# Gate weights' sums by adding DMAs issued by GpSimd instead of VectorE additions

## The reference, cut to what matters

```python
proj = jnp.einsum('bsd,df->bsf', h, w_in[l])          # h: 512 x 2048
gates = jax.nn.sigmoid(parts[9 + 3 * n_g] + gate_b[l]) # the last 3 * 2048 columns of proj
```

## Time and profile before

| what | value |
|---|---|
| median of three runs | 2642.93 us |
| the profiled execution's own time | 2641.48 us |
| its span | 2639.7 us |
| TensorE busy | 2616.3 us (99%) |
| VectorE busy | 1554.9 us (59%) |
| ScalarE busy | 866.8 us (33%) |
| GpSimd busy | 0.2 us |
| share of PE in the chain that ended last | 95% |
| DMA | 359.41 MB, 136 GB/s over the span |

### The profile page before, as it was taken

One profiled execution on the slowest core, in us unless ns is written; L12 is line 12 of the kernel. 1 busy time (PEld: TensorE's weight loads), 2 busy tenths in 40 slices (PEclk: granted clock), 3 DMA queues, 4 the chain that ended last, 5 costly groups with the idle time before them and its releaser, 6 DMA issues.

```text
span 2639.7 us, 31265 instructions
## 1 busy us (share of the span) xinstructions
PE 2616.3 (99%) x12030; PEld 2162.5 (82%) x12030; DVE 1554.9 (59%) x1911; ACT 866.8 (33%) x1089; POOL 0.2 (0%) x4
## 2 busy tenths in 40 slices
PE   9999999999999999999999999999999999999998
PEld 7888888888888888888888888878888888888776
DVE  7653654554455455365455446798877784444775
ACT  6222332322222233232232223334444443212454
POOL 0000000000000000000000000000000000000000
PEclk9999999999999999999999999999999999999999
DMA  6333333332332432333334243435455436444565
GB/s 220 120 92 126 97 118 97 120 124 91 124 132 84 131 116 89 112 108 123 93 120 131 84 132 124 139 114 186 168 190 177 164 131 247 160 144 143 189 190 195
DMA packets 102825, 359.41 MB, mean 136 GB/s; under 512 B 10017, under 2 KB 10274, under 8 KB 100770
## 3 DMA queue, kind: packets, MB, share of 16 engines
q1 hardware_dynamic: 82352, 296.49, 34.2%
q10 hardware_dynamic: 20338, 60.89, 6.3%
HBM read 317.50 MB, written 39.85 MB: 135 GB/s over the span
## 4 chain that ended last, share of the span: by engine, by line
PE 95%; DVE 3%; DMA 1%; issue 1%; SPq 0%; ACT 0%; DVEq 0%; ACTq 0%
PE proj L421 22%; PE proj L423 22%; PE proj L422 22%; PE sc_ps L421 3%; PE sc_ps L422 3%; PE sc_ps L423 3%; PE tr_ps L421 3%; PE tr_ps L422 3%; PE tr_ps L423 3%; PE o_ps L422 2%; PE o_ps L423 2%; PE o_ps L421 2%; PE tr_ps L462 2%; PE sc_ps L454 1%; DVE w_lo L1019 1%; PE o_ps L507 1%
## 5 line engine op out<-in xcount | busy, mean ns | idle before, releaser
L421 PE MATMUL proj<-act_hi,w_hi 128*128 128x512 f32 x2304 | 908.1, 394 | 0.5 <-DVE stage L1146 0.2
L423 PE MATMUL proj<-act_hi,w_lo 128*128 128x512 f32 x2304 | 898.2, 390 | 0.0
L422 PE MATMUL proj<-act_lo,w_hi 128*128 128x512 f32 x2304 | 897.2, 389 | 0.0
L1015 DVE TENSOR_TENSOR w_lo<-raw,w_hi 128x1024 fp32r<-128x1024 f32 x288 | 352.7, 1225 | 396.4 <-ACT w_hi L703 395.9
L703 ACT ACTIVATE w_hi<-raw 128x1024 fp32r<-128x1024 f32 x288 | 304.6, 1058 | 837.3 <-PE proj L423 832.3
L423 PEld LDWEIGHTS proj<-act_hi,w_lo 128*128 128x128 f32 x2304 | 432.5, 188 | 91.4
L421 PEld LDWEIGHTS proj<-act_hi,w_hi 128*128 128x128 f32 x2304 | 432.8, 188 | 89.2 <-issue 1.1
L422 PEld LDWEIGHTS proj<-act_lo,w_hi 128*128 128x128 f32 x2304 | 433.0, 188 | 86.3
L1019 DVE TENSOR_TENSOR w_lo<-raw,w_hi 128x1024 fp32r<-128x1024 f32 x152 | 185.7, 1223 | 219.2 <-ACT w_hi L707 218.9
L707 ACT ACTIVATE w_hi<-raw 128x1024 fp32r<-128x1024 f32 x152 | 161.2, 1061 | 353.3 <-PE proj L423 149.9
L707 ACT ACTIVATE w_hi<-kb 128x1024 fp32r<-128x1024 f32 x120 | 127.2, 1061 | 185.8 <-PE proj L423 65.4
(11 more groups left out here) (297 smaller groups left out, 3354.5 us busy)
## 6 DMA issues: line engine op xcount, KB each, us to landing
raw<-wst SPq DMA_DIRECT2D x288, 512.0 KB, 3.5
raw<-wg SPq DMA_DIRECT2D x48, 512.0 KB, 4.0
raw<-wb SPq DMA_DIRECT2D x48, 512.0 KB, 3.6
kb<-wg SPq DMA_DIRECT2D x10, 2048.0 KB, 7.6
ssum<-wo ACTq DMA_DIRECT2D x8, 2048.0 KB, 10.5
s_dram<-ssum ACTq DMA_DIRECT2D x8, 2048.0 KB, 7.5
raw<-s_dram SPq DMA_DIRECT2D x32, 512.0 KB, 3.4
kb<-wg SPq DMA_DIRECT2D x24, 512.0 KB, 5.9
```

The costliest lines, as they stand in the source:

```text
L421: nc.tensor.matmul(out, w_h, a_h, start=first, stop=False, skip_group_check=shared)
L422: nc.tensor.matmul(out, w_h, a_l, start=False, stop=False, skip_group_check=shared)
L423: return nc.tensor.matmul(out, w_l, a_h, start=False, stop=last, skip_group_check=shared)
L1015: tt(w_lo[slot_w][:, :], raw[slot_raw][:, :], w_hi[slot_w][:, :].bitcast(f32), ALU.subtract).then_inc(lo_done, 1)
```

## The change

The three areas become two. `sum_a` (at the place of the old `k1`) is loaded with W22; GpSimd then issues DMAs that add a unit of a weight from HBM onto it in place: W21 (giving R1), after R1's split W11 (R2), after R2's split W12 (R4). `sum_b` (at the place of the old `k3`) is loaded with W21, and W11 is added (R3). These are 16 adding DMAs of 512 KB a quad, 96 in all, and VectorE's 96 additions are gone. W11, the operand of product 0, comes through the ring, so the ring carries 12 units a quad in place of 8. All loads are now single units of 512 KB; the first quad's are issued by SP behind `o_ready`, `sum_a` and `sum_b` ahead of the ring, and ScalarE issues none.

```diff
+RING_G = 3 * NU
+X_B = RING_G * QUADS_G
...
-def summed(kind, q, u):
-    return 16 * q + 4 * kind + u + 1
+def summed(kind, q):
+    return 16 * {R1: 3 * q + 1, R2: 3 * q + 2, R4: 3 * q + 3, R3: q + 1}[kind]
...
-        k2, k3, k1 = [[kb[:, 4096 * n + HU * u:4096 * n + HU * (u + 1)] for u in range(NU)] for n in range(3)]
+        sum_a, sum_b = [[kb[:, 4096 * n + HU * u:4096 * n + HU * (u + 1)] for u in range(NU)] for n in (2, 1)]
...
                 elif x < X_B + RING:
-                    q, n = divmod(x - RING, 8)
-                    if n < NU:
-                        sp.wait_ge(sum_done, summed(R4, q, n))
-                    else:
-                        sp.wait_ge(lo_done, R_G + STEPS * q + 24 + n - NU + 1)
+                    q, n = divmod(x - RING, RING_G)
+                    sp.wait_ge(lo_done, R_G + STEPS * q + 12 * (n // NU) + n % NU + 1)
...
             for u in range(NU):
-                load_k1(0, u)
+                load_a(0, u)
+            for u in range(NU):
+                load_b(0, u)
             for q in range(QUADS_G):
-                for u in range(3):
-                    load_12(q, u)
+                for n in range(NU):
+                    load_part(q, n, W11)
                 if q:
                     sp.wait_ge(got, evicted(q - 1, 6, 1))
                 sp.dma_start(rows[:, 0:2 * C], rows_d[0:1, 2 * C * q:2 * C * (q + 1)].to_broadcast([P, 2 * C])).then_inc(brow_in, 16)
-                sp.wait_ge(sum_done, summed(R2, q, NU - 1))
-                if q < QUADS_G - 1:
-                    sp.dma_start(kb[:, 0:4096], wg[q + 1, W22, :, :]).then_inc(k2_in, 16)
-                else:
+                for n in range(NU, 2 * NU):
+                    load_part(q, n, W12)
+                if q == QUADS_G - 1:
                     for b in range(3):
                         sp.wait_ge(y_stored[b], 16 * (HEADS + 1))
                     load_y(0)
-                load_12(q, 3)
-                for u in range(3):
-                    load_22(q, u)
+                for n in range(2 * NU, 3 * NU - 1):
+                    load_part(q, n, W22)
                 if q < QUADS_G - 1:
-                    sp.wait_ge(lo_done, R_G + STEPS * q + 20)
-                    sp.dma_start(kb[:, 4096:8192], wg[q + 1, W21, :, :]).then_inc(k3_in, 16)
+                    for u in range(NU):
+                        sp.wait_ge(lo_done, R_G + STEPS * q + 16 + u + 1)
+                        load_b(q + 1, u)
                     for u in range(NU):
                         sp.wait_ge(lo_done, R_G + STEPS * q + 20 + u + 1)
-                        load_k1(q + 1, u)
-                load_22(q, 3)
+                        load_a(q + 1, u)
+                load_part(q, 3 * NU - 1, W22)
...
+        @block.gpsimd
+        def _(pool):
+            def sum_units(q, kind):
+                buf, part, done = {R1: (sum_a, W21, a_sum), R2: (sum_a, W11, a_sum), R4: (sum_a, W12, a_sum), R3: (sum_b, W11, b_sum)}[kind]
+                for u in range(NU):
+                    if kind == R1:
+                        pool.wait_ge(a_in[u], 16 * (q + 1))
+                    elif kind == R3:
+                        pool.wait_ge(b_in[u], 16 * (q + 1))
+                    else:
+                        pool.wait_ge(lo_done, R_G + STEPS * q + {R2: NU, R4: 2 * NU}[kind] + u + 1)
+                    pool.dma_start(buf[u], wg[q, part, :, HU * u:HU * (u + 1)], accum_op=ALU.add).then_inc(done[u], 16)
+
+            for q in range(QUADS_G):
+                sum_units(q, R1)
+                sum_units(q, R2)
+                sum_units(q, R3)
+                sum_units(q, R4)
...
-                    if n < 4:
-                        add_units(R3, q, n)
-                    if 4 <= n < 8:
-                        add_units(R2, q, n - 4)
-                    if 12 <= n < 16:
-                        add_units(R4, q, n - 12)
-                    if 24 <= n and q < QUADS_G - 1:
-                        add_units(R1, q + 1, n - 24)
```

More of the change, by code:

```diff
@@ L62 @@
 R_O = R_B + GROUPS * NU
-X_B = 8 * QUADS_G
+RING_G = 3 * NU
+X_B = RING_G * QUADS_G
 X_O = X_B + GROUPS * NU
@@ L244, in program @@
         raw_in = [sem(f"raw_in{i}") for i in range(RING)]
-        k1_in = [sem(f"k1_in{i}") for i in range(NU)]
-        k2_in, k3_in = sem("k2_in"), sem("k3_in")
+        a_in, b_in = [[sem(f"{n}_in{i}") for i in range(NU)] for n in "ab"]
+        a_sum, b_sum = [[sem(f"{n}_sum{i}") for i in range(NU)] for n in "ab"]
         brow_in, grow_in = sem("brow_in"), sem("grow_in")
@@ L267, in program @@
         th_ready, sq_ready, sd_ready, y_ready = sem("th_ready"), sem("sq_ready"), sem("sd_ready"), sem("y_ready")
-        sum_done, got, gate_done = sem("sum_done"), sem("got"), sem("gate_done")
+        got, gate_done = sem("got"), sem("gate_done")
         comb_sum, comb_hi, comb_lo = sem("comb_sum"), sem("comb_hi"), sem("comb_lo")
@@ L318, in ring_free, with load_part, load_a, load_b @@
                 elif x < X_B + RING:
-                    q, n = divmod(x - RING, 8)
-                    if n < NU:
-                        sp.wait_ge(sum_done, summed(R4, q, n))
-                    else:
-                        sp.wait_ge(lo_done, R_G + STEPS * q + 24 + n - NU + 1)
+                    q, n = divmod(x - RING, RING_G)
+                    sp.wait_ge(lo_done, R_G + STEPS * q + 12 * (n // NU) + n % NU + 1)
                 else:
                     sp.wait_ge(lo_done, R_B + x - RING - X_B + 1)
[L327 to L336, removed]
+            def load_part(q, n, kind):
+                ring_free(RING_G * q + n)
+                load_ring(RING_G * q + n, wg[q, kind, :, HU * (n % NU):HU * (n % NU + 1)])
+            def load_a(q, u):
+                sp.dma_start(sum_a[u], wg[q, W22, :, HU * u:HU * (u + 1)]).then_inc(a_in[u], 16)
+            def load_b(q, u):
+                sp.dma_start(sum_b[u], wg[q, W21, :, HU * u:HU * (u + 1)]).then_inc(b_in[u], 16)
             def load_y(b):
@@ L716, in hi_g @@
                 r = R_G + STEPS * q + n
[L717 to L722, removed]
+                if p == 1:
+                    act.wait_ge(a_sum[u], summed(R1, q))
+                    hi_of(r, sum_a[u])
                 elif p == 2:
-                    act.wait_ge(sum_done, summed(R2, q, u))
-                    hi_of(r, k1[u])
+                    act.wait_ge(a_sum[u], summed(R2, q))
+                    hi_of(r, sum_a[u])
                 elif p == 4:
-                    act.wait_ge(sum_done, summed(R3, q, u))
-                    hi_of(r, k3[u])
+                    act.wait_ge(b_sum[u], summed(R3, q))
+                    hi_of(r, sum_b[u])
                 elif p == 5:
-                    act.wait_ge(sum_done, summed(R4, q, u))
-                    hi_of(r, k1[u])
+                    act.wait_ge(a_sum[u], summed(R4, q))
+                    hi_of(r, sum_a[u])
                 else:
-                    hi_ring(r, 8 * q + (u if p == 3 else NU + u))
+                    hi_ring(r, RING_G * q + NU * (p // 3) + u)
             def comb_high(n, dst, src, ready):
@@ L839, in head @@
                         exps(i, 4 + w - 10, sc, [(0, 6 * P)], SCALE_B)
[L840 to L844, removed]
                     if w in (AZ, BZ, CZ):
@@ L1023, in lo_g @@
                 p, u = divmod(n, NU)
-                src = (k1[u], k2[u], k1[u], raw[(8 * q + u) % RING][:, :], k3[u], k1[u], raw[(8 * q + NU + u) % RING][:, :])[p]
+                src = {1: sum_a[u], 2: sum_a[u], 4: sum_b[u], 5: sum_a[u]}.get(p, raw[(RING_G * q + NU * (p // 3) + u) % RING][:, :])
                 lo_of(R_G + STEPS * q + n, src)
[L1027 to L1043, removed]
             def comb_low(dst, whole, hi, n):
@@ L1226, in head @@
                         norm_b(i, w - 11)
-                    if last and w == 17:
-                        for n in range(NU):
-                            add_units(R1, 0, n)
                     if not (fresh and w < 2):
```

## The result

The changed kernel takes 2685.21 us (median of four runs, 2683.26 to 2688.33), the kernel before beside it 2643.72: slower, ratio 1.0158 with a 95% interval of 1.014 to 1.0175. That is 41.5 us; the two profiled executions differ by 41.8 in span (2681.5 against 2639.7).

What follows compares the result with a forecast made beforehand. The prediction took PE, busy 99%, to bound the kernel. Profiled execution 2641.5, entry +1 and boundaries +30 gave 2672.5; with medians 1.4 above, 2674, rounded to 2673 us; range 2635 to 2745.

Steps and rivals of the forecast that it cites:

- the likeliest case: Gates stage: a full DMA system delays the quads' ends; 2673 us, its own range 2650 to 2710, chance 0.40.
- What bounds the kernel: Whole kernel: PE, busy 99% of the span; in the gates stage it loses time only at the entry, 9.1 us.
- VectorE's additions in later quads: Five later quads: 80 of the 96 additions lie beside a full PE, so removing them is worth 0.
- The price: Each adding DMA: moves its unit twice through the same engines, so costs a factor of 2 against a plain load.
- The entry: Start of the gates: VectorE's relief against W11's later landing through the ring; -6.5, -1 or +4 us, taken as +1.
- Priced once: Start of the gates: R1's four additions cost the engines what plain loads do, so W11 lands at 1733.6.
- The boundaries: Five quad ends, where ring loads and R1 share the engines: about 6 us late each, 30 us.
- DMA pace sets the time then: Quad ends: full DMA engines set the time, 30.0 MB a quad at 379 GB/s, so a lowered clock adds little.
- The signs named beforehand: A quad's stretch: DMA share near 1.0 and 80 to 84 us if right; 75.8 us with share under 0.9 if wrong.
- bias and W12: SP's queue: what stands behind the ring's fourth W11 unit, which waits for unit 0; none wanted before unit 12.
- Waits added: Gates stage: R2 is tight, 4.9 us a doubled transfer against 8.5 us available; holds unless the queue is full.
- Rival 2: Entry: additions cost little and W11 lands by 1729, so 6 to 7 us come back; 2636 us, chance 0.14.

Runs made afterwards that it cites:

- ring_first: Changed kernel with SP's first two W11 units issued ahead of sum_a and the other two between sum_a and sum_b: 2673.88 us (1.0111).
- plain_loads: Changed kernel with GpSimd's 96 adding DMAs made plain loads of the same units at the same places, sums left out: 2647.02 us (1.0007).
- r1_vector: Changed kernel with `ring_first` and `y_early` edits, and R1 of quads 1 to 5 made by VectorE: 2642.13 us (0.999).
- y_early: Changed kernel with the first y block's load ahead of W12's four units in SP's program for the last quad: 2676.2 us (1.012).
- hybrid3: Kernel before, with R1, R2 and R3 of the first quad alone made by adding DMAs (12 in all): 2637.52 us (0.9972).

## Why the prediction came out as it did

The time (2673 forecast, 2685 measured, in the range) and the side were right, and so was the likeliest case's place, the DMA side at the quads' ends; its cause was not. That the time came so near is in part luck: the boundaries were put 7 us too high, the entry 6 too low, and a loss of 12 was missing. Its steps:

- **What bounds the kernel, and that VectorE's additions in later quads are worth 0:** right. PE is the bound in every kernel whose transfers arrive.
- **The price, a factor of 2:** right, 1.93 in the kernel and 1.9 alone. The Trainium skill ("Collectives: The Full Stack", The bandwidth ceiling) gives a measured ratio of 1.93 between a gathering and a reducing collective; these runs agree: 397 GB/s of loads against 210 of adding DMAs is a factor of 1.9.
- **The entry, "-6.5, -1 or +4", taken as +1:** mis-sized. ScalarE's first gate unit went at 1740.3; the doubled price gave 1739, and at that price the step said +4. I had weakened it to +1 for a sharing that might be unequal; 7.1 was measured, and 7.0 to 9.7 in kernels that are alike there. So even +4 was too small: unit 4's low part began at 1759.78 where the step had 1757.6, 8.3 us after the kernel before, and of these 8.3 only 1.2 came back by unit 20 instead of 2, as ScalarE then waited for R2's additions (1.9 and 1.4 us) and a ring unit (3.7). That W11's place is the cause is shown by `ring_first`. Priced once, W11 was forecast at 1733.6; `plain_loads` has 1735.6 there and +2.1.
- **The boundaries, "5 quad boundaries x 6 = 30 us":** size near (22.8), place right (the quad's end, R1 beside the ring), cause wrong. "DMA pace sets the time then", with the mean of 30.0 MB against 379 GB/s, fell: with 12 additions a quad the loss stays if R1 is among them and goes if it isn't. I had taken the queues' sharing as by bytes; it goes by turns, in which the loads pay for the dearer additions beside them. The signs named beforehand didn't tell the two apart: the quad took 80.4 us (80 to 84 was named) with a DMA share of 0.99, but `r1_vector` has 75.8 us a quad with 0.92.
- **What the prediction lacked:** the first y load, 11.8 us. It named what stands behind the fourth W11 unit on SP as "bias and W12", not the load further behind, which now waits for a ring unit until unit 12 is split. `y_early` shows it.
- **Waits added, R2 tight but holding:** right but for little. ScalarE waits for R2's additions (41.3 us in 20 waits), yet of the 22.8 us at the boundaries all but 0.6 is there before R2's units begin, and `r1_vector` has 18.7 us of these waits up to 2115 us and no loss in four quads.
- **Rival 2, a gain at the entry alone:** its mechanism is real (`hybrid3`), its place in the changed kernel was taken by the late W11.

What stays open: the 7.0 to 9.7 us of the entry in kernels that are alike there, where the start-up differences of the first ten units come from, and whether a packet or a descriptor is the turn that the queues take; the runs show only that units progress one for one. No kernel was run with R1's additions alone left on GpSimd, so that they suffice for the whole loss isn't shown, only that the loss needs them; nor how much of the 4.6 us would remain if the full engines at a quad's end shared by bytes.

## What to carry to other kernels

Relieve an engine only where the bound engine waits for it: here the 12 additions moved in `hybrid3`, of the first quad, gave all of the gain, the other 84 gave nothing, and the 20 of R1 in the later quads cost some 4.6 us for each four. In these runs an adding DMA was paid twice, once by itself and once by every load that took turns with it, so compare the time between landings with the pace at which a small ring is consumed, not the bytes of a long stretch with the peak. And when a program in order gets longer waits, follow everything behind them to the end of that queue's list.

## What of the hardware I had not expected

Queues of unlike transfers share by turns, not by bytes. With 8192 bytes for descriptors, 16 loads that last about 21 us alone (16 x 1.3) last 60 beside 16 adding DMAs that last about 40 alone (16 x 2.5), and the queues end 5 us apart at a nearly constant 275 GB/s. The room for GpSimd's descriptors bounds how many of its DMAs are on their way (adding DMAs at 140 instead of 210 GB/s with 1024 instead of 8192 bytes) when nothing else fills the engines; in the full kernel twice the room gained nothing (2686.87 against 2685.21 us). At the entry of the kernel before, two waits of PE of 4.7 us in all went with a loss of 9.1, most of the rest lying in matmuls at the lower of the two granted levels behind each wait (0.63 us instead of 0.39); with 1.7 us of waits the clock stayed at 1.00.

And one execution can start up to 4 us later than another in its first ten units, as the first column of the table shows, so a few us between two profiled executions are read stage by stage, not by their spans.
